# Token norm and router in one stage, tokens turned while the experts are chosen, semaphores cleared by four engines

## What is computed

```python
h = modulate(rms_norm(x, norm_ffn_g), sh2, sc2)          # x*rsqrt(mean x^2) * g * (1+sc) + sh
logits = h @ w_router + b_router
top_logit, top_idx = lax.top_k(logits, 4);  top_p = softmax(top_logit)
...
gu = xb @ w_gu[e] + b_gu[e]                               # for each expert e, on its tokens xb
act = glu * sigmoid(1.702 * glu) * (lin + 1.0)            # glu, lin: clipped halves of gu
y += (act @ w_down[e] + b_down[e]) * p
```

## Time and profile before

| | |
|---|---|
| median of 3 runs | 3371.61 us (3368.02 to 3374.78) |
| the profiled execution, its own time | 3370.95 us |
| its span from first to last instruction | 3369.1 us |
| TensorE busy | 3095.3 us, 92% of the span |
| VectorE busy | 2133.0 us, 63% |
| ScalarE busy | 1614.5 us, 48% |
| experts' products, about | 1236 to 2383 us of the span |

### The profile page before, as it was taken

How to read it: one execution, slowest core, us unless ns; L and a number is a source line. 1 busy time by engine, 2 the same in 40 slices (tenths; PEclk the granted TensorE clock), 3 DMA queues, 4 the chain that set the end, 5 groups by cost and what they waited for, 6 DMA issues and landing times. The chain is left out here.

```text
span 3369.1 us, 45314 instructions
## 1 busy us (share of the span) xinstructions
PE 3095.3 (92%) x17512; PEld 2565.3 (76%) x17513; DVE 2133.0 (63%) x3271; ACT 1614.5 (48%) x2238; POOL 143.4 (4%) x175
## 2 busy tenths in 40 slices
PE   7989999988887969999999999999597799997998
PEld 2558888855566958888788788788496699985998
DVE  2135455534444569988898998988566466564664
ACT  0024444411113447777777777777343245442453
POOL 0032232200000000000000000000000000000000
PEclk9899999987777969999999999999797599995899
DMA  7450110011114469999999999999161055540463
GB/s 263 140 90 26 40 37 1 1 40 38 37 37 144 144 252 338 358 350 342 349 359 336 353 358 337 356 355 339 44 198 54 19 165 174 151 138 0 127 183 117
DMA packets 261717, 605.63 MB, mean 180 GB/s; under 512 B 26018, under 2 KB 86665, under 8 KB 261385
## 3 DMA queue, kind: packets, MB, share of 16 engines
q1 hardware_dynamic: 260428, 602.40, 52.2%
q10 hardware_dynamic: 1085, 0.45, 0.0%
HBM read 598.39 MB, written 4.39 MB: 179 GB/s over the span
## 5 line engine op out<-in xcount | busy, mean ns | idle before, releaser
L1840 DVE TENSOR_TENSOR moe_raw_r<-moe_raw,moe_hi 128x2048 fp32r<-128x2048 f32 x320 | 720.2, 2284 | 14.8 <-ACT moe_hi L1778 14.8
L1778 ACT ACTIVATE moe_hi<-moe_raw 128x2048 fp32r<-128x2048 f32 x320 | 599.9, 1907 | 102.8 <-PE banks L1702 102.6
L2564 PE MATMUL banks<-xs_r,w_hi 128*128 128x272 f32 (+1 forms) x1632 | 475.7, 292 | 25.5 <-DVE w_raw_r L2986 16.9
L2568 PE MATMUL banks<-xs_r,w_raw_r 128*128 128x272 f32 (+1 forms) x1632 | 473.1, 290 | 0.0
L2565 PE MATMUL banks<-xs_r,w_hi 128*128 128x272 f32 (+1 forms) x1632 | 470.8, 288 | 0.0
L2808 ACT ACTIVATE w_hi<-w_raw 128x512 fp32r<-128x512 f32 (+1 forms) x416 | 256.8, 619 | 246.6 <-PE banks L2568 202.9
L1702 PE MATMUL banks<-moe_raw_r,moe_xs 128*128 128x512 f32 x1024 | 346.7, 422 | 0.0
L2564 PEld LDWEIGHTS banks<-xs_r,w_hi 128*128 128x128 f32 x1632 | 311.8, 191 | 30.6 <-issue 22.6
L2568 PEld LDWEIGHTS banks<-xs_r,w_raw_r 128*128 128x128 f32 x1632 | 311.8, 191 | 3.0
L2565 PEld LDWEIGHTS banks<-xs_r,w_hi 128*128 128x128 f32 x1632 | 312.2, 191 | 0.2
L2986 DVE TENSOR_TENSOR w_raw_r<-w_raw,w_hi 128x512 fp32r<-128x512 f32 (+1 forms) x416 | 271.3, 675 | 57.1 <-ACT w_hi L2808 53.0
(11 more groups left out here) (476 smaller groups left out, 5349.3 us busy)
## 6 DMA issues: line engine op xcount, KB each, us to landing
moe_raw<-in_w_gu SPq DMA_DIRECT2D x256, 1024.0 KB, 9.5
moe_raw<-in_w_down SPq DMA_DIRECT2D x128, 1024.0 KB, 10.6
w_raw<-in_w_ff SPq DMA_DIRECT2D x256, 256.0 KB, 3.0
w_raw<-in_w_in SPq DMA_DIRECT2D x112, 256.0 KB, 2.7
ring_mod<-in_w_mod SPq DMA_DIRECT2D x12, 2048.0 KB, 8.0
wq<-in_w_in SPq DMA_DIRECT2D x32, 512.0 KB, 4.3
wh<-in_w_in SPq DMA_DIRECT2D x10, 1024.0 KB, 9.0
mg_raw<-in_w_in SPq DMA_DIRECT2D x32, 256.0 KB, 3.2
```

The lines of the kernel that those rows point to most:

```text
L1778: act.activation(hi[n % HI_SLOTS][:, :], raw[n % UNITS][:, :], ACT.Copy).then_inc(his, 1)
L1840: dve.tensor_tensor(rest[n % UNITS][:, :], raw[n % UNITS][:, :], hi[n % HI_SLOTS][:, :].bitcast(F32), ALU.subtract).then_inc(los, 1)
L2564: pe.matmul(bank, w_hi, x[:, 0, 0:n_cols], start=first, stop=False)
L2568: ins = pe.matmul(bank, w_lo, x[:, 0, 0:n_cols], start=False, stop=last)
```

## The change

Five things are changed.

- Every clearing block, of `stage()` and of `clear_all()`, deals its semaphores to VectorE, ScalarE, TensorE and SyncE in turn.
- The norm's stage and the router's stage become one with 11 semaphores. One barrier pair and its clearing go. SyncE's loads stand at the head of the merged stage. The two elementwise passes over the 8 slices become one VectorE operation per slice (x times gain times reciprocal) and one ScalarE operation per slice that adds the shift; TensorE's logit products wait slice by slice.
- TensorE turns the tokens back directly after the logit products, before it waits for `sel`.
- The 4 bias products move from the end of the router's stage into the experts' stage, after the first unit of expert 0. Their operands `bd` and `gT` now lie in `y_tok` and `pickT`, which live on into that stage.
- ScalarE rounds the first 3 units before it copies the gathered tokens, instead of after.

```diff
@@ def stage
         with nc.Block(no_gpsimd_drain=True) as block:
+            every = [*sems, *held]
+
             @block.vector
             def _(dve):
-                for s in (*sems, *held):
+                for s in every[0::4]:
                     dve.sem_clear(s)
+            @block.scalar
+            def _(act):
+                for s in every[1::4]:
+                    act.sem_clear(s)
+            @block.tensor
+            def _(pe):
+                for s in every[2::4]:
+                    pe.sem_clear(s)
+            @block.sync
+            def _(sp):
+                for s in every[3::4]:
+                    sp.sem_clear(s)
@@ def experts
                 for q in range(4):
                     unit("g", 0, q)
+                    if q == 0:
+                        for t in range(2):
+                            for c in range(2):
+                                pe.matmul(ps[4 + 2 * t + c][:, :], gT[:, t * P:(t + 1) * P], bd[:, c * 512:(c + 1) * 512],
+                                          start=True, stop=False)
...
                 act.preload_act_table(ACT.Sigmoid)
+                for n in range(3):
+                    rounded(n)
                 x_of(0)
-                for n in range(8):
+                for n in range(3, 8):
                     rounded(n)
@@ def route
-        rsqrt_stage(nc, "ffn", ps[0], lambda k: xT[:, k, :], KT, LAT, LAT, ones, sq, rinv[:, :], D)
-        with stage(nc, "r_w r_v r_mm r_act r_h_act r_split") as (block, w_in, on_dve, mm, on_act, h_act, h_split):
+        with stage(nc, "r_w r_v r_mm r_act r_h_act r_sq r_sum r_var r_std r_inv r_h2") as \
+                (block, w_in, on_dve, mm, on_act, h_act, squared, summed, var, std, inv, h2_act):
...
                 v(dve.tensor_scalar(gain[:, :], modT[:, 4 * KT:5 * KT, 0], 1.0, None, ALU.add))
+                for k in range(KT):
+                    dve.tensor_tensor(sq[:, k, :], xT[:, k, :], xT[:, k, :], ALU.mult).then_inc(squared, 1)
                 v.wait()
                 v(dve.tensor_tensor(gain[:, :], gain[:, :], vec[:, V_FFN:V_FFN + KT], ALU.mult))
-                for k in range(KT):
-                    v(dve.tensor_tensor(h2T[:, k, :], xT[:, k, :], rinv[:, :], ALU.mult))
+                dve.wait_ge(summed, 1)
+                dve.tensor_scalar(rinv[:, :], ps[0][:, 0:LAT], 1.0 / D, EPS, ALU.mult, ALU.add).then_inc(var, 1)
+                dve.wait_ge(std, 1)
+                dve.reciprocal(rinv[:, :], rinv[:, :]).then_inc(inv, 1)
+                dve.wait_ge(inv, 1)
                 v.wait()
                 for k in range(KT):
-                    v(dve.tensor_scalar(h2T[:, k, :], h2T[:, k, :], gain[:, k:k + 1], modT[:, 3 * KT + k, 0:1], ALU.mult, ALU.add))
+                    v(dve.scalar_tensor_tensor(h2T[:, k, :], xT[:, k, :], gain[:, k:k + 1], rinv[:, :], ALU.mult, ALU.mult))
...
             def _(act):
+                act.preload_act_table(ACT.Sqrt)
+                act.wait_ge(var, 1)
+                act.activation(rinv[:, :], rinv[:, :], ACT.Sqrt).then_inc(std, 1)
+                for k in range(KT):
+                    act.wait_ge(on_dve, 2 + k + 1)
+                    act.activation(h2T[:, k, :], h2T[:, k, :], ACT.Identity,
+                                   bias=modT[:, 3 * KT + k, 0:1]).then_inc(h2_act, 1)
...
             def _(pe):
-                pe.wait_ge(on_dve, 18)
+                for k in range(KT):
+                    pe.wait_ge(squared, k + 1)
+                    ins = pe.matmul(ps[0][:, 0:LAT], ones, sq[:, k, :], start=(k == 0), stop=(k == KT - 1))
+                ins.then_inc(summed, 1)
                 pe.wait_ge(w_in, 48)
+                pe.wait_ge(var, 1)
                 for t in range(2):
                     for k in range(KT):
+                        pe.wait_ge(h2_act, k + 1)
                         ins = pe.matmul(ps[0][:, t * E_N:(t + 1) * E_N], h2T[:, k, t * P:(t + 1) * P], wr[:, k, :],
                                         start=(k == 0), stop=(k == KT - 1))
                 ins.then_inc(mm, 1)
+                for t in range(2):
+                    for k in range(KT):
+                        ins = pe.transpose(ps[3 + 2 * t + k // 4][:, k % 4 * P:(k % 4 + 1) * P], h2T[:, k, t * P:(t + 1) * P], ident)
+                    ins.then_inc(mm, 1)
                 pe.wait_ge(on_dve, SEL_AT)
...
-                pe.wait_ge(on_dve, GT_AT)
-                pe.wait_ge(h_split, 2)
-                for t in range(2):
-                    for c in range(2):
-                        pe.matmul(ps[4 + 2 * t + c][:, :], gT[:, t * P:(t + 1) * P], bd[:, c * 512:(c + 1) * 512],
-                                  start=True, stop=False)
```

More of the change, by code:

```diff
@@ L174, in _ @@
         def _(dve):
-            for s in sems:
+            for s in sems[0::4]:
                 dve.sem_clear(s)
+        @block.scalar
+        def _(act):
+            for s in sems[1::4]:
+                act.sem_clear(s)
+        @block.tensor
+        def _(pe):
+            for s in sems[2::4]:
+                pe.sem_clear(s)
+        @block.sync
+        def _(sp):
+            for s in sems[3::4]:
+                sp.sem_clear(s)
 def rsqrt_stage(nc, tag, ps, src, tiles, n, width, ones, sq, rinv, mean_of, eps=EPS):
@@ L1623, in experts @@
         gate = sb("gate", [P, 2, E_N])
+        pickT = sb("pickT", [2 * SLOTS, LAT])
+        y_sb, acs = both_types(ctx, nc, "y_tok", [P, KT, 2 * SLOTS])
+        y = y_sb[:, :, :].rearrange("p k n -> p (k n)")
+        bd, gT = y[0:E_N, :], pickT[0:E_N, :]
         flags = sb("flags", [1, NJ], mybir.dt.int32)
@@ L1638, in first_units @@
                 load_unit(sp, n)
-        route(nc, a, ps, con, vec, xT, modT, ident, ones, h_hi, h_lo, rankr, gate, flags, items, first_units)
+        route(nc, a, ps, con, vec, xT, modT, ident, ones, h_hi, h_lo, rankr, gate, flags, items, bd, gT, first_units)
         hi = [sb(f"moe_hi{s}", [P, 16 * P], FR) for s in range(HI_SLOTS - 1)]
@@ L2130, in _, with route @@
                 ins.then_inc(summed, 1)
-def route(nc, a, ps, con, vec, xT, modT, ident, ones, h_hi, h_lo, rankr, gate, flags, items, first_units):
+def route(nc, a, ps, con, vec, xT, modT, ident, ones, h_hi, h_lo, rankr, gate, flags, items, bd, gT, first_units):
     RMAX = LAT // SLOTS
@@ L2145, in route @@
         br = sb("br", [P, E_N])
-        bd = sb("bd", [E_N, D])
         lg = sb("lg", [P, 2, E_N])
@@ L2218, in _ @@
                 assert v.n == GATE_AT
-                dve.wait_ge(mm, 2)
+                dve.wait_ge(mm, 4)
                 v(dve.scalar_tensor_tensor(lg[:, :, :], ps[1][:, 0:2 * E_N].rearrange("p (t e) -> p t e", t=2), 1.0, sel[:, :, :],
@@ L2253, in _ @@
                 for t in range(2):
-                    act.wait_ge(mm, 3 + t)
+                    act.wait_ge(mm, 2 + t)
                     act.activation(h_hi[:, t, :].rearrange("p (b n) -> p b n", b=2), ps.all[:, 3 + 2 * t:5 + 2 * t, :],
@@ L2273, in _ @@
                 pe.matmul(ps[2][:, 0:E_N], ones, sel[:, 1, :], start=False, stop=True).then_inc(mm, 1)
-                for t in range(2):
-                    for k in range(KT):
-                        ins = pe.transpose(ps[3 + 2 * t + k // 4][:, k % 4 * P:(k % 4 + 1) * P], h2T[:, k, t * P:(t + 1) * P], ident)
-                    ins.then_inc(mm, 1)
                 pe.wait_ge(on_dve, GATE_AT)
@@ L2281, in _ @@
                 ins.then_inc(mm, 1)
-                pe.wait_ge(on_dve, GT_AT)
-                pe.wait_ge(h_split, 2)
-                for t in range(2):
-                    for c in range(2):
-                        pe.matmul(ps[4 + 2 * t + c][:, :], gT[:, t * P:(t + 1) * P], bd[:, c * 512:(c + 1) * 512],
-                                  start=True, stop=False)
-PR_AT = 24
+PR_AT = 16
 SEL_AT = PR_AT + 1 + TOP + 3
```

6 lines of the change are left out of this document (1 added, 5 removed).

## The result

The changed kernel took 3325.29 us (median of 4 runs, 3323.51 to 3327.14), the kernel before on the same chip 3371.06 (4 runs, 3368.02 to 3374.78): a ratio of 0.9862, with a 95% interval of 0.9847 to 0.9878. The prediction was 3342.6 with a range from 3332 to 3359.

A forecast was written before the change was run, and what follows sets the result against it. The prediction took TensorE, busy 92% of the span, as the bound, outright in the experts' stage. Clears 18.6 plus norm and router 13.8 minus start of the experts' stage 3.8 made 28.6 us gained: 3342.6, range 3332 to 3359.

The forecast's parts named there:

- From there on TensorE is the bound, and all moves with it: Experts' stage from expert 0's second half on: TensorE sets the time, so earlier gains or losses carry through; no further term.
- Rival 3: Experts' stage: the clock is granted less; at 0.91 the 1120 us become 1145, total 3367; chance 0.05.
- Clears: Clearing blocks between barriers: dealing clears to four engines gains 18.6 us, with TensorE's clear at 0.113 us.
- Rivals 1 and 4: Clearing blocks. 1: four engines' clears queue up, 3361.5, chance 0.10. 4: TensorE's clear is slow, 3379 at 0.55 us, chance 0.02.
- Router: Norm and router, up to the experts' first `pick`: that `pick` comes 13.8 us sooner.
- Rival 5: The router's part brings nothing because the experts wait for their weights: 3352, chance under 0.01.
- Start of the experts' stage: From the first `pick` to expert 0's second half: 27.8 us against 24.0, so 3.8 lost.
- So I take 7.15 for them: Bias products after expert 0's first unit: granted clock stays at 0.50, so they take 7.15 us.
- rival 2: Start of the experts' stage: the clock rises ahead of the bias products, 5.4 us more gained, 3337; chance 0.25.

The follow-up runs named there:

- e3: The changed kernel with y_tok and pickT allocated late again and the bias operands in gu_tok instead: 3331.56 us, ratio 0.9889.
- e2: The kernel before with only y_tok and pickT allocated ahead of the weight units, no instruction changed: 3349.95 us, ratio 0.9947.
- e11_slot: The kernel before with one line moved, gate_slot (32 bytes) allocated behind y_tok instead of ahead of moe_xs: 3337.75 us median.
- e5: The changed kernel with moe_xs also allocated early, right behind y_tok, ahead of the weight buffers: 3306.15 us, ratio 0.9818.
- e1: The kernel before with only the clears dealt to VectorE, ScalarE, TensorE and SyncE: 3348.7 us, ratio 0.9943.
- e4: The kernel before with only the merged norm and router stage and the early transposes: 3361.71 us, ratio 0.9983.
- e7: The kernel before with only three roundings ahead of the copy of the gathered tokens: 3361.6 us, ratio 0.9986.
- e6: The changed kernel with the bias products behind the fourth unit of expert 0 instead of the first: 3318.59 us, ratio 0.9856.
- e12: The kernel of e5 with 32 bytes of padding ahead of y_tok, shifting weights' tiles and moving units together: 3299.55 us (one run).
- e13: The kernel of e12 with 96 more bytes behind moe_xs, so only the weights' tiles are shifted: 3338.05 us (one run).

## Why the prediction was wrong

**The step that failed** is "From there on TensorE is the bound, and all moves with it", with the operands that "now lie in `y_tok` and `pickT`", which had no term in the sum. To make them live into the experts' stage the change allocates `y_tok` early. That took away the 32 bytes by which it stood off the moving units, and the second layer's products got some 6.5 ns shorter each. The expert loop takes 1106.4 us instead of 1117.6. The 11.2 us come in two parts: 32 products of each of 32 experts at 6.5 ns make at most 6.7, and the rest is the clock, since the time at 1.2 GHz in the loop fell from 167 to 157 us. In e3 this part of the gain went away with the tile's place, and in e2 and e11_slot it came with no instruction changed. That shorter experts also get less time at 1.2 GHz was seen in every such run (154 us in e2, 140 in e5 and e11_slot), and never with long ones (167 or more); why is not shown. Rival 3 had looked to this clock, but for a loss that a shift in time would bring; the shift did nothing (e1, e4, e7).

**Clears**: predicted 18.6, 19.2 with the two small blocks counted in the router. Without those two the clearing blocks, from one barrier to the next, gave 17.0. The mechanism was right, the price 0.117 to 0.119 for TensorE instead of 0.113, and blocks of a few clears gained less than was reckoned (0.13 us for four). Rivals 1 and 4 are out.

**Router**: predicted 13.8, measured 14.9 (34.4 to 19.4). Each step stands where it was put; the ranks ran partly at the high clock. It was a gain of the chain together: the merged stage by itself gave 6.4 (e4), because there the bias products still stood behind it, and most of the other part of the 14.9 is their 7.15 us. Rival 5 is out: the first expert product waited for the copy of the tokens, not for weights.

**Start of the experts' stage**: predicted 3.8 lost, measured 1.0 lost. The first product at 8.7 was exact, and e7 shows the roundings' gain by itself (4.5 us by the medians). Mis-sized was "So I take 7.15 for them": the clock rose one microsecond into the bias products and they took 4.17. That is between the forecast and rival 2, and the clock fell back behind them, which neither had. All in all moving them gains 7.15 in the router and costs 24.5 - 18.6 = 5.9 behind it; behind the fourth unit (e6) they cost 3.3.

**The sum as it was**: clears 17.0, router 14.9, start -1.0, loop 11.2, together 42.1 of the span's 47.4. Of the other 5.3, some 3.7 lie in the stages ahead of the norm, the rest mainly behind the experts. Those stages, with unchanged work, differ by as much between other runs (2 less in e2, 5 less in e1, clears apart), with other stretches at 1.2 GHz; no run ties it to a part of the change. The prediction's sum also has a slip: 3371.61 - 28.6 is 3343.0, not 3342.6, which changes nothing.

## What to carry to other kernels

When TensorE is the bound, compare where the weights' tile and the moving tile start in a partition before and after any change of allocation: here one 32-byte tile ahead of them cost 31 us of 3368, and no view of waits showed it, only the mean of each group of products. Read the means of groups whose code is untouched first: they tell whether the gain comes from where you think. Work that moves into a stage at a low clock is best put where the clock is already up and a wait can hide it.

## What the runs showed of the hardware

- Products of 512 columns of rounded 32-bit data that load 128 x 128 weights: at 2.4 GHz one starts every 227 ns where the weights' tile starts a multiple of 512 bytes from the moving units (changed kernel, e5, e11_slot, e12), and every 233 ns where it starts 32 bytes past a multiple of 128 from them (before, e3, e13). Other distances were not run. At 1.2 GHz one starts every 426 ns in either case.
- A semaphore clear has a pitch of 0.084 us on VectorE, 0.067 on ScalarE, 0.056 on SyncE and 0.117 on TensorE. VectorE's pitch was no longer with four engines clearing at once than alone.
- Bias products with 32 rows: the clock fell to 0.50 behind them in the changed kernel, after 3.4 us at 1.00, and stayed at 1.00 behind them in e6, where full products had run at 1.00 for 4.6 us ahead.
